# Modulation rows in four column groups of TensorE, and most of norm1's tiles loaded in norm1's own stage

## The reference, cut to what matters

```
def adaln(cond, w, b):
    return jax.nn.silu(cond) @ w + b
def modulate(h, shift, scale):
    return h * (1.0 + scale) + shift
...
sh1, sc1, gt1, sh2, sc2, gt2 = jnp.split(adaln(c, w_ada[i], b_ada[i])[:, None, :], 6, axis=-1)
csh1, csc1, cgt1, csh2, csc2, cgt2 = jnp.split(adaln(c_ctx, w_ada[i], b_ada[i]), 6, axis=-1)
hc = modulate(rmsnorm(ctx, g_pre_mix[i]), csh1, csc1)
hx = modulate(rmsnorm(x, g_pre_mix[i]), sh1, sc1)
```

## Time and profile before

| | |
|---|---|
| median of 3 runs | 3549.29 us (3548.83 to 3549.63) |
| the profiled execution | 3552.48 us, its span 3550.7 us |
| TensorE matmul busy | 3108.4 us (88%) |
| VectorE busy | 2068.4 us (58%) |
| ScalarE busy | 1329.2 us (37%) |
| GpSimd busy | 328.5 us (9%) |
| mean granted TensorE clock | 0.932 |
| DMA over the whole span | 424.23 MB, 119 GB/s |

### The profile page before, as it was taken

How to read it: one execution, slowest core, us unless ns; L and a number is a source line. 1 busy time by engine, 2 the same in 40 slices (tenths; PEclk the granted TensorE clock), 3 DMA queues, 4 the chain that set the end, 5 groups by cost and what they waited for, 6 DMA issues and landing times. The chain is left out here.

```text
span 3550.7 us, 57598 instructions
## 1 busy us (share of the span) xinstructions
PE 3108.4 (88%) x24401; PEld 2433.2 (69%) x24401; DVE 2068.4 (58%) x2561; ACT 1329.2 (37%) x1767; POOL 328.5 (9%) x231
## 2 busy tenths in 40 slices
PE   6899957799999999788988888777999958999995
PEld 2687746588888788655575766666666736888884
DVE  4443355666666444455567676676211367888885
ACT  2211243311211233346344343434110225777774
POOL 2000011100000000211020211120000000222210
PEclk7899978899999999899998999888999978999997
DMA  4442003211111332202002020102210447999996
GB/s 174 155 154 76 25 19 127 88 48 47 47 47 47 134 105 100 83 7 78 20 3 69 3 70 2 52 3 90 56 36 24 166 167 264 390 400 394 394 398 219
DMA packets 220245, 424.23 MB, mean 119 GB/s; under 512 B 13362, under 2 KB 122884, under 8 KB 219780
## 3 DMA queue, kind: packets, MB, share of 16 engines
q1 hardware_dynamic: 214418, 401.56, 31.3%
q0 software_dynamic: 4608, 16.78, 1.8%
q10 hardware_dynamic: 1013, 2.86, 0.2%
HBM read 387.62 MB, written 33.55 MB: 119 GB/s over the span
## 5 line engine op out<-in xcount | busy, mean ns | idle before, releaser
L213 DVE TENSOR_TENSOR w_exp_low<-w_exp,w_exp_high 128x2048 fp32r<-128x2048 f32 x192 | 438.1, 2291 | 56.6 <-ACT w_exp_high L208 56.5
L208 ACT ACTIVATE w_exp_high<-w_exp 128x2048 fp32r<-128x2048 f32 x192 | 368.0, 1920 | 126.1 <-PE psum L221 126.0
L219 PE MATMUL psum<-ffn_high,w_high 128*128 128x512 f32 x704 | 274.0, 389 | 0.6 <-DVE w_low L213 0.6
L220 PE MATMUL psum<-ffn_low,w_high 128*128 128x512 f32 x704 | 273.9, 389 | 0.0
L221 PE MATMUL psum<-ffn_high,w_low 128*128 128x512 f32 x704 | 273.9, 389 | 0.0
L1537 DVE SCALAR_TENSOR_TENSOR ffn_hidden<-u_padded,param_columns,ffn_hidden 128x1024 f32 (+1 forms) x176 | 226.0, 1284 | 21.1 <-DVE ffn_hidden L1533 1.6
L219 PE MATMUL psum<-w_exp_high,x_turned_high 128*128 128x512 f32 x512 | 203.9, 398 | 4.4 <-DVE w_exp_low L213 4.4
L221 PE MATMUL psum<-w_exp_high,x_turned_low 128*128 128x512 f32 x512 | 201.2, 393 | 0.0
L220 PE MATMUL psum<-w_exp_low,x_turned_high 128*128 128x512 f32 x512 | 201.2, 393 | 0.0
L2524 DVE COPY inverse<-psum 64x512 f32<-64x512 f32 x192 | 121.9, 637 | 74.4 <-PE psum L2347 58.7
L2460 ACT ACTIVATE inverse<-psum 64x512 f32<-64x512 f32 x192 | 106.8, 556 | 142.8 <-PE psum L2347 108.9
(11 more groups left out here) (519 smaller groups left out, 7481.1 us busy)
## 6 DMA issues: line engine op xcount, KB each, us to landing
w_exp<-in_exp_w_gate SPq DMA_DIRECT2D x32, 2048.0 KB, 11.0
w_exp<-in_exp_w_up SPq DMA_DIRECT2D x32, 2048.0 KB, 11.2
w_exp<-in_exp_w_down SPq DMA_DIRECT2D x32, 2048.0 KB, 10.4
w_raw<-in_w_up SPq DMA_DIRECT2D x44, 512.0 KB, 3.7
ffn_down_ring<-in_w_down SPq DMA_DIRECT2D x44, 512.0 KB, 3.5
ada_weights_late<-in_w_ada SPq DMA_DIRECT2D x16, 1024.0 KB, 5.8
mix_out_ring<-in_w_out SPq DMA_DIRECT2D x32, 512.0 KB, 4.2
mixers_hT<-hidden SPq DMA_DIRECT2D x4, 4096.0 KB, 13.9
```

The source lines that it names most:

```text
L208: return nc.scalar.activation(out, src, ACT.Copy, scale=scale)
L213: return nc.vector.tensor_tensor(out, src, high.bitcast(F32), ALU.subtract)
L219: nc.tensor.matmul(out, left[0], right[0], start=start, stop=False)
L220: nc.tensor.matmul(out, left[0], right[1], start=False, stop=False)
```

## The change

Four k of a block go to four groups of 32 columns of the array, each with its own 32 partitions of the bank; a group adds up two of the eight. The stationary operand is therefore padded with zeros from 2 to 32 columns (`padded`, cleared by GpSimd and filled by a ScalarE copy). The bias stands in partitions 0 and 1 of a cleared tile of 128; it is issued after the Silu and that copy. The bias sum and the spread work on all 128 partitions, so that the spread also adds the four groups: its selecting operand takes from the identity mask, by a sum over the four groups (`sums`), the partitions that carry condition v. SP loads only tiles 0 and 1 of x in "mod". "norm1" gets a list `fetch`: SP issues tile 2, tiles 3 and 4, tiles 5 to 7, and ctx, and ScalarE waits for each before its first square.

```diff
+    select = core.at("select_row", 109, [P, 2, P])
+    padded = core.at("cond_padded", 110, [P, KD, 32])
+    sums = core.at("select_sums", 111, [P, 2])
+    pairs = core.at("row_pairs", 178, [P, NW, 512])
+    bias = core.at("ada_bias", 186, [P, 2 * D])
...
+            nc.gpsimd.memset(padded[:], 0.0).then_inc(cleared, 1)
+            nc.gpsimd.memset(bias[:], 0.0).then_inc(cleared, 1)
             nc.gpsimd.memset(ones[:], 1.0).then_inc(ones_done, 1)
...
-            sp.dma_start(core.x0[:], dram["x"][0].rearrange("(t p) d -> p t d", p=P)).then_inc(x_in, 16)
-            sp.dma_start(core.ctx[:], dram["ctx"][0].rearrange("(t p) d -> p t d", p=P)).then_inc(ctx_in, 16)
+            sp.dma_start(core.x0[:, 0:2], dram["x"][0].rearrange("(t p) d -> p t d", p=P)[:, 0:2]).then_inc(x_in, 16)
...
-            act.dma_start(bias[:], dram["b_ada"][:, 0:2 * D].to_broadcast([2, 2 * D])).then_inc(bias_in, 16)
             act.wait_ge(cond_in, 32)
             nc.scalar.activation(csil.ap().rearrange("p k v -> p v k"), cvec[:], ACT.Silu).then_inc(silu_done, 1)
+            act.wait_ge(silu_done, 1)
+            act.wait_ge(cleared, 1)
+            nc.scalar.activation(padded[:, :, 0:2], csil[:], ACT.Copy).then_inc(pad_done, 1)
+            act.wait_ge(cleared, 2)
+            act.dma_start(bias[0:2, :], dram["b_ada"][:, 0:2 * D].to_broadcast([2, 2 * D])).then_inc(bias_in, 16)
...
+            nc.vector.reduce_sum(sums[:], core.mask(M_ID).rearrange("p (g r) -> p r g", r=32)[:, 0:2, :], axis=AX
+                                 ).then_inc(sums_done, 1)
+            dve.wait_ge(sums_done, 1)
             for v in range(2):
-                nc.vector.tensor_copy(select[:, v, :], core.masks[0:2, M_ID, v:v + 1].to_broadcast([2, P])
-                                      ).then_inc(selects, 1)
+                nc.vector.tensor_copy(select[:, v, :], sums[:, v:v + 1].to_broadcast([P, P])).then_inc(selects, 1)
...
-                nc.vector.tensor_tensor(pairs[:, j], ps[0:2, j, :], bias[:, 512 * j:512 * j + 512], ALU.add
+                nc.vector.tensor_tensor(pairs[:, j], ps[:, j, :], bias[:, 512 * j:512 * j + 512], ALU.add
...
-                    ins = nc.tensor.matmul(ps[0:2, j, :], csil[:, k, :], ada_w[:, j, k], start=(k == 0),
-                                           stop=(k == KD - 1))
+                    g = k % 4
+                    ins = nc.tensor.matmul(ps[32 * g:32 * g + 32, j, :], padded[:, k, :], ada_w[:, j, k], start=(k < 4),
+                                           stop=(k >= 4), tile_position=(0, 32 * g))
...
+                for n, (first, _, _) in enumerate(fetch):
+                    if first == t:
+                        act.wait_ge(fetched[n], 16)
                 nc.scalar.activation(junk[:], tiles[t][0], ACT.Square, accum_out=stat[:, 0, t:t + 1]
...
+            for n, (_, dst, src) in enumerate(fetch):
+                sp.dma_start(dst, src).then_inc(fetched[n], 16)
...
+                    fetch=[(t, core.x0[:, t:t + n], x_tiles[:, t:t + n]) for t, n in ((2, 1), (3, 2), (5, 3))]
+                    + [(TT, core.ctx[:], dram["ctx"][0].rearrange("(t p) d -> p t d", p=P))])
```

More of the change, by code:

```diff
@@ L246, in stage_modulation @@
     ones = core.ones = core.at("ones", 9, [P, P])
-    select = core.at("select_row", 109, [2, 2, P])
-    pairs = core.at("row_pairs", 178, [2, NW, 512])
-    bias = core.at("ada_bias", 186, [2, 2 * D])
+    select = core.at("select_row", 109, [P, 2, P])
[3 more added lines that the diff above has]
+    bias = core.at("ada_bias", 186, [P, 2 * D])
     graw = core.at("gain_rows", 150, [P, D])
@@ L254, in stage_modulation @@
     with Stage(core, "mod") as s:
-        (masks_in, x_in, ctx_in, cond_in, param_in, bias_in, gain_in, silu_done, ones_done, selects, params_turned,
+        (masks_in, x_in, cond_in, param_in, bias_in, gain_in, silu_done, ones_done, selects, params_turned,
          params_out, pair_mm, pair_done, spread, shifts_done, gains_done) = s.sems(
-            "masks_in", "x_in", "ctx_in", "cond_in", "param_in", "bias_in", "gain_in", "silu_done", "ones_done", "selects",
+            "masks_in", "x_in", "cond_in", "param_in", "bias_in", "gain_in", "silu_done", "ones_done", "selects",
             "params_turned", "params_out", "pair_mm", "pair_done", "spread", "shifts_done", "gains_done")
         w_in = [s.sem(f"w_in{j}") for j in range(NW)]
+        cleared, pad_done, sums_done = s.sems("cleared", "pad_done", "sums_done")
         n_par = sum(len(t) for t in PARAM_ROWS)
@@ L329, in _ @@
             dve.wait_ge(x_in, 16)
-            dve.wait_ge(ctx_in, 16)
         @s.b.tensor
@@ L340, in spread_rows @@
                                      ).then_inc(spread, 1)
-            pe.wait_ge(silu_done, 1)
+            pe.wait_ge(pad_done, 1)
             pe.wait_ge(selects, 2)
@@ L357, in _, with stage_norm_turn @@
             spread_rows(NW - 1)
-def stage_norm_turn(core, name, jobs, scratch_kb, store=None, load=(), ready=0, ahead=()):
+def stage_norm_turn(core, name, jobs, scratch_kb, store=None, load=(), ready=0, ahead=(), fetch=()):
     nc, ps = core.nc, core.psum
@@ L383, in stage_norm_turn @@
         ready_stored = s.sem("ready_stored")
+        fetched = [s.sem(f"fetched{n}") for n in range(len(fetch))]
         def rows_of(t):
@@ L1571, in first_block @@
     core.hT_ctx = (core.at("mix_ctx_high", 76, [P, KD, CT], F32R), core.at("mix_ctx_low", 12, [P, KD, CT], F32R))
+    x_tiles = dram["x"][0].rearrange("(t p) d -> p t d", p=P)
     stage_norm_turn(core, "norm1", [(core.x0, TT, rows[:, R_G1], rows[:, R_SH1], core.hT_x, 0),
-                                    (core.ctx, CTT, rows[:, R_CG], rows[:, R_CSH], core.hT_ctx, 0)], 150)
+                                    (core.ctx, CTT, rows[:, R_CG], rows[:, R_CSH], core.hT_ctx, 0)], 150,
+                    fetch=[(t, core.x0[:, t:t + n], x_tiles[:, t:t + n]) for t, n in ((2, 1), (3, 2), (5, 3))]
+                    + [(TT, core.ctx[:], dram["ctx"][0].rearrange("(t p) d -> p t d", p=P))])
     stage_project_mix(core)
```

## The result

The change saved 21.6 us in its first comparison: 3527.67 us (3523.62 to 3533.67, 5 executions) against 3549.29, ratio 0.9948 with the interval 0.9937 to 0.9959. Forecast were 3536.3 us, 13.0 less, with a range of 3533 to 3543. The direction was right; the time lies 5 us under the range. Two later comparisons of the same pair gave less: 13.8 us (ratio 0.9954, 0.9940 to 0.9967) and 12.7 us (0.9959, 0.9943 to 0.9975). The mean of the three differences is 16.0 us. The profiled execution took 3523.62 us (span 3521.8), the fastest of its five. One execution in the whole document, 3819.44 us at a mean granted clock of 0.806 in experiment 7, stood far from all others of its kernel and is left out.

A forecast was written before the change was run, and what follows sets the result against it. TensorE's group matmuls were taken to bound the first stage. Tail shift 14.6 less 0.3 for loads and 1.0 for clock gave 13.3, rounded to 13.0 us: 3549.3 to 3536.3 us, range 3533 to 3543.

The forecast's parts named there:

- The bound and the main term: First stage: TensorE's group matmuls set its end; four column groups cut a block from 6.9 to 1.7 us, leaving DMA bound.
- The shift of the tail: First stage, behind block 3: that block ends at 33.5 instead of 48.1 us, so everything after moves 14.6 us earlier.
- The moved loads, 0.3 us: Norm1: tile 2 lands late by 0.1 to 0.8 us, less the slack; cost 0.3 us, later loads none.
- The clock, 1.0 us: First stage: gaps before blocks 2 and 3 may drop TensorE's clock; cost 1.0 us, bounds 0 and 2.6.
- Rival B: First stage: gaps keep TensorE's clock at half throughout, the end moves only 5.8 us, time 3543.5 us; chance 0.12.
- the saving carries over: Whole kernel: the opening's saving, rounded to 13.0 us, comes off the median of 3549.3 us, giving 3536.3.
- rival E: Later stages: clock phases return part of the gain, up to 2.6 us each; two or more leave 3542 or more; chance 0.05.
- Rivals C and D: C: groups run one after another, 3549.5 us, chance 0.06. D: norm1 becomes bound by its loads, 3554, chance 0.02.

The follow-up runs named there:

- experiment 7: The changed kernel with 15.9 us of GpSimd memsets behind the last gains, against the kernel before: 3550.09 us against 3550.21, ratio 0.9997.
- Experiment 6: The changed kernel with tiles 0 to 3 of x issued before the last block of weights, norm1 fetching from tile 4: one execution, 3545.41 us.
- Experiments 1 and 2: Unedited repeats: the kernel before beside itself, 3549.72 us against 3547.96, ratio 1.0003; then the changed kernel again, 3534.13 us, ratio 0.9954.

## Why the prediction was right and where it failed

**The bound and the main term: right.** The blocks went from 6.9 to 1.7 us in step, and weights now release them. Without the moved loads the stage ends with ctx at 44.17 (forecast 44.4).

**The shift of the tail: 14.6 forecast, 15.6 measured.** The last block started at 31.0 instead of the 31.8 taken, because its weights landed earlier, at 30.96 against 31.71 before. In three profiles without the groups they landed at 31.53 to 31.78, in six with the groups and the same order of weights at 30.82 to 31.44. Bias, gains and parameters are issued later there; whether that is the reason was not tested. The other 0.3 us is a shorter way from the last spread but one to the stage's end (5.54 us against 5.82), most of it in the parameter turning. The repeat profiles give the same end within 0.5 us (38.40, 38.47, 38.87).

**The moved loads, 0.3 us: nothing.** Tile 2 came in 3.3 us from issue, under both rows used; in a repeat it was 0.17 us late and that lay in the slack too. Tile 3's lateness of 0.60 us (0.88 and 0.67 in the repeats) lay in its slack, as worked out.

**The clock, 1.0 us: nothing.** The only fall came where the prediction had called it covered. Experiment 6 confirms its price at 2.4 us. Rival B's condition did not hold: from 23.4 us to the stage's end the clock was 1.00. So for the opening the sum was 13.3, rounded to 13.0, and the measurement 15.6: the terms for losses were each taken above their floor, and none occurred.

**The step that failed: that the saving carries over, with rival E and the range.** The prediction took the saving of the opening over to a median of three runs that lay within 0.8 us, as if all later stages kept their length. For the phases of later stages it left 1.7 us of gain in the range (3534.7 with no loss, 3533 as its end) and made their loss a rival with a chance of 0.05. No run shows later stages that keep their length. Experiments 1 and 2 show that single executions of one kernel lie up to 19 us apart, and medians of five or more several: 21.6, 13.8 and 12.7 us of saving for one pair of kernels, 3439.5 to 3454.6 us for the same stages in profiles of the same kernel. The mis-sized terms of the opening alone would not have missed: 3549.3 - 15.6 = 3533.7 lies in the range. The first comparison held 6 us more than the opening, and that was luck, since neither repeat had it. That these 6 us lay in later stages is inferred: the profile that shows 13.2 us there is of the fastest execution, and the median one has none. Its five executions (3523.62 to 3533.67) overlap ten later ones of the same kernel (3527.22 to 3538.82). Rivals C and D are excluded by the blocks' length and by norm1's 43.99 us.

**What stays open.** Why the last weights land earlier, why the clock falls in one execution's scan and not in another's, and why 1 MB lands in 6.6 or 8.5 us was not found; the correlation over twelve profiles does not say which comes first.

## What to carry to other kernels

Here a thin matmul (few stationary columns) on fp32 went to a quarter of its time, because its k were dealt to four column groups and the selecting matmul that follows summed them. In such a case look first where the weights' DMA then stands, because behind it the next bound waits: here x and ctx, worth 5.8 us only after the groups. Size a small change by its stage, from one opening to the next, and its time by repeated comparisons: three runs within 0.8 us said nothing of a spread of 19.

## What the runs showed of the hardware

Four column groups of 32 ran fully in parallel, a step of four records with 512 fp32 columns each in 0.43 us at full clock; two groups of 64 took twice as many such steps (3.65 us a block against 1.92). The granted clock stayed at 1.00 over gaps of TensorE of 1.57 us, and of 1.74 with two groups. It fell with gaps of 2.45 and 2.79 us, when the next block had already begun, 3.0 us into a gap of 3.25, and 4.6 us into one of 6.45. After that last fall 5.0 us of continuous work ran at half before it rose. On one core and with the same instructions, the stages from attention through the scan took 916.5 to 929.6 us in twelve profiles.
